# All gate matmuls of an attention step in one block, between the transposes of its two pairs

## The chip, the cores and the metric

One core of a Trainium2 chip runs the whole program. The metric is the device time of one execution in microseconds (us). TensorE (PE) does the matmuls and the transposes, ScalarE (ACT) and VectorE (DVE) the element-wise work, SyncE (SP) and GpSimd (POOL) issue transfers. The loads of the stationary operand are recorded apart from the matmuls, as PEld. Engines run their own instruction lists in order and wait for each other on semaphores.

## What is computed

One layer of a transformer on 128 context tokens and 512 latent tokens, model width 1024. Cut to what matters here:

```
u = h @ w_in  -> A: q(8 heads) k,v(2 heads) | B: q,k,v(8 heads) | gate_A | gate_B
ya = attention A   (window of +-128 tokens, a sink logit, keys of the cache)
yb = attention B   (8 x 16 neighbourhood on the 64-wide grid with a bias, keys of the cache)
merge = (sigmoid(gate_A) * (ya @ w_out_a) + sigmoid(gate_B) * (yb @ w_out_b)) @ w_o
x = x + gate1 * merge;  x = x + gate2 * SwiGLU(...)
```

The gates need only h and their columns of w_in, so their matmuls can stand anywhere before the merge. This kernel puts most of them into the attention, as work for TensorE while the other engines do the softmax.

## The kernel before, in words

The attention is a list of 40 pairs (`PAIRS`). A pair is one mixer, one tile of two heads (`hh` = 0 and 1) and one block of 128 queries. Mixer A has the first 20 pairs, mixer B the last 20. Two pairs make a step, a = 2i and b = 2i + 1, so there are 20 steps (`N_STEPS`); the text counts them from 1 to 20. For each pair:

- `scores` (L2378), TensorE: queries by keys into PSUM. It is run two steps ahead.
- `negate_scores` (L1610), VectorE: mask or bias, negated, and the row minimum.
- `exp` (L1072), ScalarE; then `normalise` (L1618 reciprocal, L1622 scaling of the two heads), VectorE.
- `transposes` (L2390), TensorE: each head's probabilities are turned, in blocks of 128 keys: 1, 3 or 4 blocks by the pair. The blocks of one head go into one PSUM bank (4 + hh). It waits for `norm_done` of the head, and for `pt_done` of the pair before it, since that pair used the same bank.
- `copy_pt` (L1080), ScalarE: one copy per head from PSUM to SBUF, which signals `pt_done`.
- `outputs` (L2406), TensorE: probabilities by values. Each head's first matmul waits for its `pt_done`. `take_output` (L1090, L1094) on ScalarE copies the result.

The gate matmuls are cut into chunks `(g, half, k)` of three matmuls 128x320 (L2418). `GATE_STEPS[i]` says which chunks belong to step i: 4 chunks in 14 steps and 8 in 6 steps (numbers 3, 8, 13, 16, 19 and 20). When a half of a gate is complete, ScalarE takes it with `take_gate` (L1062).

The order on each engine is written out by hand. TensorE's is the loop below, ScalarE's in one step is: two copies of a, one `exp` of the next step's a, two copies of b, two more `exp`, the gate if one is complete, the last `exp`, the two outputs, and in six steps a 1.06 us split of weights (L887). So the copies of b stand behind an `exp` that itself waits for VectorE, and three `exp` of the next step stand behind the copies of b. VectorE does in one step the four `negate_scores` of the next step, `normalise` of its two pairs, in most steps one or two parts of a modulation sum (L1464), and in six steps a split (L1413).

TensorE's loop in the kernel before (L2433 to L2446):

```
for i in range(N_STEPS):
    a, b = 2 * i, 2 * i + 1
    n = len(GATE_STEPS[i]) // 2
    transposes(a)
    for chunk in GATE_STEPS[i][:n]: gate_chunk(*chunk)
    transposes(b)
    for chunk in GATE_STEPS[i][n:]: gate_chunk(*chunk)
    outputs(a); outputs(b)
    if i + 2 < N_STEPS: scores(a + 4); scores(b + 4)
```

The numbers of blocks of pairs a and b come from `value_parts`. Over the 20 steps they are (a, b): (1, 4) in steps 1 and 6, (3, 4) in 2 and 7, (1, 3) in 11 and 16, (3, 3) in 5, 10, 12, 14, 15, 17, 19 and 20, (4, 1) in 3 and 8, (4, 3) in 4 and 9, (3, 1) in 13 and 18.

Of the kernel before, what the change touches and what calls it, by code (L numbers as in the profile page):

```python
# [230 lines left out]
def hybrid_dit_program(nc, x_t, c_t, w_ada1, w_ada, w_main, vecs, consts, cache_ka,  # L231
# [6 lines left out]
    with ctx:  # L238
# [293 lines left out]
        GATE_STEPS, CHUNKS = [], [(g, half, k) for g in range(N_GATE_ATT) for half in range(2) for k in range(KT)]  # L532
# [1631 lines left out]
        def _(pe):  # L2164
# [202 lines left out]
            def scores(p):  # L2367
                mixer, t, blk = PAIRS[p]
                if p >= 2:
                    pe.wait_ge(ttr_done, 2 * p - 2)  # L2370

                parts = [score_parts(mixer, t, blk, hh) for hh in range(2)]
                tile = (QA if mixer == "A" else QB) + t
                for c in range(len(parts[0])):
                    for hh in range(2):
                        rows = slice(hh * HD, (hh + 1) * HD)
                        at, keys = parts[hh][c]
                        ins = pe.matmul(ps[:, 2 * (p % 2) + hh, at:at + keys.shape[1]], qk[rows, tile, blk * P:(blk + 1) * P],  # L2378
                                        keys, start=True, stop=True)
                        if c == len(parts[0]) - 1:  # L2380
                            ins.then_inc(score_done, 1)

            def transposes(p):
                for hh in range(2):
                    r = 2 * p + hh
                    if p:
                        pe.wait_ge(pt_done, r - 1)
                    pe.wait_ge(norm_done, r + 1)
                    for c, (at, n, _) in enumerate(value_parts(*PAIRS[p], hh)):
                        ins = pe.transpose(ps[0:n, 4 + hh, c * P:(c + 1) * P], e_sb[r % 8][:, at:at + n], ident)  # L2390
                    ins.then_inc(t_done, 1)

            def outputs(p):

                parts = [value_parts(*PAIRS[p], hh) for hh in range(2)]
                if p >= 2:
                    pe.wait_ge(o_done, p // 2 * 2)
                if p == FIRST_B:
                    pe.wait_ge(v_in, 16 * 3)
                    pe.wait_ge(pool_set, 2)  # L2400
                for c in range(len(parts[0])):
                    for hh in range(2):
                        if c == 0:
                            pe.wait_ge(pt_done, 2 * p + hh + 1)
                        _, n, v = parts[hh][c]
                        ins = pe.matmul(ps[hh * HD:(hh + 1) * HD, 6, p % 2 * P:(p % 2 + 1) * P], v,  # L2406
                                        pt_sb[PAIRS[p][0]][p % 2][hh][0:n, c * P:(c + 1) * P],
                                        start=c == 0, stop=c == len(parts[0]) - 1)
                ins.then_inc(pv_done, 1)

            def gate_chunk(g, half, k):
                if k == 0:
                    if not half:
                        pe.wait_ge(lo_done, U_GATE + g + 1)
                    pe.wait_ge(act_read, N_ACC + 2 * g + half)
                w = slice(k * P, (k + 1) * P)
                for n, (wt, rt) in enumerate(((w_hi, h_hi), (w_hi, h_lo), (w_lo, h_hi))):
                    ins = pe.matmul(ps[:, 7, 0:TH], wt[:, (U_GATE + g) % RING, w], rt[:, k, half * TH:(half + 1) * TH],  # L2418
                                    start=k == 0 and n == 0, stop=k == KT - 1 and n == 2)
                if k == KT - 1:  # L2420
                    ins.then_inc(pe_unit if half else first_half, 1)
# [10 lines left out]
            scores(3)  # L2432
            for i in range(N_STEPS):  # L2433
                a, b = 2 * i, 2 * i + 1
                n = len(GATE_STEPS[i]) // 2
                transposes(a)
                for chunk in GATE_STEPS[i][:n]:
                    gate_chunk(*chunk)
                transposes(b)
                for chunk in GATE_STEPS[i][n:]:  # L2440
                    gate_chunk(*chunk)
                outputs(a)
                outputs(b)
                if i + 2 < N_STEPS:
                    scores(a + 4)
                    scores(b + 4)  # L2446
# [313 lines left out]
```

## Time and profile before

| what | us |
|---|---|
| median of 3 runs (894.14 to 897.92) | 894.8 |
| the profiled execution, its own time | 894.82 |
| its span in the trace | 893.0 |
| PE busy / DVE busy / ACT busy | 877.5 / 706.5 / 468.0 |
| the attention, from the first scores to the last outputs | 164.6 to 298.0 |

Busy time of PE counts overlapping matmuls as they are drawn in the trace, so it hides small gaps. How densely TensorE works is seen better in the starts of its weight loads (PEld rows): one starts per matmul, 0.146 us apart in a gate block. A row's columns are start, duration (from the first start to the last end, when several instructions are merged), engine, line, operation, operands, count, and in brackets the idle time before it and what ended that.

### The profile page before, as it was taken

How to read it: one execution, taken by the hardware profiler on the slowest of the kernel's cores; microseconds unless marked ns; L12 is line 12 of the kernel's file. 1: busy time of each engine (PE TensorE's matmuls, PEld its weight loads, DVE VectorE, ACT ScalarE, POOL GpSimd, SP SyncE). 2: the span in 40 equal slices, each digit the busy share in tenths (PEclk: the TensorE clock that was granted, in tenths of full speed). 3: DMA queues.
4: the chain of work that ended last, by engine and by line, in shares of the span. 5: the costliest groups of instructions: out<-in, count | busy, mean ns of one | idle time of the engine just before them, and what ended most of it. 6: DMA issues, size and time to landing. Idle time of an engine off the chain costs nothing. (4 is left out here: it accounts for less than half of the span.)

```text
span 893.0 us, 16552 instructions
## 1 busy us (share of the span) xinstructions
PE 877.5 (98%) x6235; PEld 833.9 (93%) x6235; DVE 706.5 (79%) x1330; ACT 468.0 (52%) x973; POOL 122.3 (14%) x155
## 2 busy tenths in 40 slices
PE   6999999999999999999999999999999999999998
PEld 5689888898889999999998999999999999999997
DVE  4657899799788499774777968997777998778887
ACT  4763444777777533432246734555444555545553
POOL 0000000010000000000000123223333222333221
PEclk9999999999999999999999999999999999999999
DMA  9954344441453220228305478878989886898867
GB/s 366 364 190 166 139 141 143 143 134 62 153 157 117 72 71 1 78 112 328 120 24 214 98 163 188 189 168 195 204 190 201 189 188 164 193 214 188 183 150 146
DMA packets 51663, 145.32 MB, mean 163 GB/s; under 512 B 6000, under 2 KB 12416, under 8 KB 50176
## 3 DMA queue, kind: packets, MB, share of 16 engines
q1 hardware_dynamic: 32000, 102.38, 34.8%
q0 software_dynamic: 18864, 41.11, 24.1%
q8 instruction: 50, 0.82, 0.4%
q10 hardware_dynamic: 720, 0.77, 0.3%
q14 instruction: 29, 0.24, 0.1%
HBM read 121.68 MB, written 12.20 MB: 150 GB/s over the span
## 5 line engine op out<-in xcount | busy, mean ns | idle before, releaser
L1318 ACT ACTIVATE w_hi<-stage 128x512 fp32r<-128x512 f32 (+1 forms) x186 | 106.0, 608 | 98.4 <-DMA stage<-stage 47.8
L2009 DVE TENSOR_TENSOR w_lo<-stage,w_hi 128x512 fp32r<-128x512 f32 (+1 forms) x186 | 117.7, 668 | 25.2 <-ACT w_hi L1318 24.9
L2608 PE MATMUL ps<-m_hi,w_hi 128*128 128x320 f32 x304 | 93.9, 309 | 0.0
L2608 PE MATMUL ps<-m_lo,w_hi 128*128 128x320 f32 x304 | 93.9, 309 | 0.0
L2608 PE MATMUL ps<-m_hi,w_lo 128*128 128x320 f32 x304 | 93.9, 309 | 0.0
L2608 PE MATMUL ps<-h_hi,w_hi 128*128 128x320 f32 x272 | 84.0, 309 | 0.0
L2608 PE MATMUL ps<-h_lo,w_hi 128*128 128x320 f32 x272 | 84.0, 309 | 0.0
L2608 PE MATMUL ps<-h_hi,w_lo 128*128 128x320 f32 x272 | 84.0, 309 | 0.0
L887 ACT ACTIVATE w_hi<-stage 128x1024 fp32r<-128x1024 f32 x47 | 49.6, 1064 | 62.2 <-PE ps L2278 36.9
L2608 PE MATMUL ps<-y_hi,w_hi 128*128 128x320 f32 x264 | 81.7, 309 | 0.0
L2608 PE MATMUL ps<-y_lo,w_hi 128*128 128x320 f32 x264 | 81.6, 309 | 0.0
L2608 PE MATMUL ps<-y_hi,w_lo 128*128 128x320 f32 x264 | 81.6, 309 | 0.0
L1413 DVE TENSOR_TENSOR w_lo<-stage,w_hi 128x1024 fp32r<-128x1024 f32 x47 | 57.2, 1221 | 30.1 <-ACT w_hi L887 29.7
L2278 PE MATMUL ps<-w_hi,h_hi 128*128 128x512 f32 (+1 forms) x200 | 75.0, 375 | 0.0
L2278 PE MATMUL ps<-w_lo,h_hi 128*128 128x512 f32 (+1 forms) x200 | 73.7, 369 | 0.0
L2278 PE MATMUL ps<-w_hi,h_lo 128*128 128x512 f32 (+1 forms) x200 | 73.7, 368 | 0.0
L2608 PEld LDWEIGHTS ps<-m_lo,w_hi 128*128 128x128 f32 x304 | 57.1, 188 | 0.0
L2608 PEld LDWEIGHTS ps<-m_hi,w_lo 128*128 128x128 f32 x304 | 57.1, 188 | 0.0
L2608 PEld LDWEIGHTS ps<-m_hi,w_hi 128*128 128x128 f32 x304 | 57.1, 188 | 0.0
L2608 PEld LDWEIGHTS ps<-h_hi,w_hi 128*128 128x128 f32 x272 | 51.1, 188 | 0.0
L2608 PEld LDWEIGHTS ps<-h_lo,w_hi 128*128 128x128 f32 x272 | 51.1, 188 | 0.0
L2608 PEld LDWEIGHTS ps<-h_hi,w_lo 128*128 128x128 f32 x272 | 51.1, 188 | 0.0
(311 smaller groups left out, 2440.0 us busy)
## 6 DMA issues: line engine op xcount, KB each, us to landing
stage<-w_main SPq DMA_DIRECT2D x118, 512.0 KB, 4.3
x<-w_ada SPq DMA_DIRECT2D x21, 512.0 KB, 4.6
stage<-stage POOLq DMA_DIRECT2D x38, 256.0 KB, 4.3
qk<-w_ada SPq DMA_DIRECT2D x7, 1024.0 KB, 12.0
scr<-w_main POOLq DMA_DIRECT2D x28, 256.0 KB, 6.1
y_t<-scr POOLq DMA_DIRECT2D x22, 320.0 KB, 6.5
s_second<-w_main POOLq DMA_DIRECT2D x26, 256.0 KB, 6.2
stage<-w_main POOLq DMA_DIRECT2D x19, 256.0 KB, 6.6
```

The source lines that it names most:

```text
L887: act.activation(w_hi[:, slot, :], stage[:, slot, :], ACT.Copy).then_inc(hi_done, 1)
L1318: act.activation(w_hi[:, slot, at:at + job_half(j) * P], left_stage(op, j), ACT.Copy).then_inc(left_hi[op], 1)
L1413: dve.tensor_tensor(w_lo[:, slot, :], stage[:, slot, :], w_hi[:, slot, :].bitcast(F32), ALU.subtract).then_inc(lo_done, 1)
L2009: dve.tensor_tensor(w_lo[:, slot, w], left_stage(op, j), w_hi[:, slot, w].bitcast(F32), ALU.subtract).then_inc(left_lo[op], 1)
L2278: ins = pe.matmul(ps[:, acc_bank(b, i), 0:width], (h_hi, h_lo)[part][:, k, i * P:(i + 1) * P], wt[:, u % RING, at:at + width], start=k == ...
L2608: ins = pe.matmul(ps[:, BANK_OF[op], 0:TH], wt[:, slot, w], right(op, part, j, k), start=k == 0 and n == 0, stop=k == half - 1 and n == 2)
```

## The change

The gate chunks of a step are no longer halved around the second pair's transposes. All of them stand between the transposes of a and the transposes of b; nothing stands between the transposes of b and the outputs. Chunks, their number per step and their order are the same.

```
@@ -2432,13 +2432,10 @@
             scores(3)
             for i in range(N_STEPS):
                 a, b = 2 * i, 2 * i + 1
-                n = len(GATE_STEPS[i]) // 2
                 transposes(a)
-                for chunk in GATE_STEPS[i][:n]:
+                for chunk in GATE_STEPS[i]:
                     gate_chunk(*chunk)
                 transposes(b)
-                for chunk in GATE_STEPS[i][n:]:
-                    gate_chunk(*chunk)
                 outputs(a)
                 outputs(b)
                 if i + 2 < N_STEPS:
```

TensorE's list in step 1, from the last matmul of the first half's gate chunks to the first matmuls of the outputs (L2418 gate matmuls, L2390 transposes, L2406 values). Before:

```order
L2418 MATMUL ps<-h_hi,w_lo 128x320
L2390 MATMUL ps<-cst,scr 128x128 x8
L2418 MATMUL ps<-h_hi,w_hi 128x320
L2418 MATMUL ps<-h_lo,w_hi 128x320
L2418 MATMUL ps<-h_hi,w_lo 128x320
L2418 MATMUL ps<-h_hi,w_hi 128x320
L2418 MATMUL ps<-h_lo,w_hi 128x320
L2418 MATMUL ps<-h_hi,w_lo 128x320
L2406 MATMUL ps<-x,va 64x128
L2406 MATMUL ps<-pt_end,va 64x128
```

After:

```order
L2418 MATMUL ps<-h_hi,w_lo 128x320
L2418 MATMUL ps<-h_hi,w_hi 128x320
L2418 MATMUL ps<-h_lo,w_hi 128x320
L2418 MATMUL ps<-h_hi,w_lo 128x320
L2418 MATMUL ps<-h_hi,w_hi 128x320
L2418 MATMUL ps<-h_lo,w_hi 128x320
L2418 MATMUL ps<-h_hi,w_lo 128x320
L2390 MATMUL ps<-cst,scr 128x128 x8
L2406 MATMUL ps<-x,va 64x128
L2406 MATMUL ps<-pt_end,va 64x128
```

The eight transposes of pair b move behind six gate matmuls, next to the outputs. The same on TensorE in step 3, where each half has twelve gate matmuls and pair b one block per head, at the end of the gate work. Before:

```order
L2418 MATMUL ps<-h_hi,w_hi 128x320
L2418 MATMUL ps<-h_lo,w_hi 128x320
L2418 MATMUL ps<-h_hi,w_lo 128x320
L2406 MATMUL ps<-x,va 64x128
L2406 MATMUL ps<-pt_end,va 64x128
```

After:

```order
L2418 MATMUL ps<-h_lo,w_hi 128x320
L2418 MATMUL ps<-h_hi,w_lo 128x320
L2390 MATMUL ps<-cst,scr 128x128 x2
L2406 MATMUL ps<-x,va 64x128
L2406 MATMUL ps<-pt_end,va 64x128
```

Here the two transposes move behind twelve gate matmuls. The lists of ScalarE, VectorE, SyncE and GpSimd are the same in both kernels, and TensorE's is the same outside the 20 steps.

## Rows read from the trace of the kernel before

**Rows 1.** The page: TensorE's busy time, and its granted clock in 40 slices.
```profile
PE 877.5 (98%) x6235; PEld 833.9 (93%) x6235; DVE 706.5 (79%) x1330; ACT 468.0 (52%) x973; POOL 122.3 (14%) x155
...
PEclk9999999999999999999999999999999999999999
```

**Rows 2.** Busy time by stretch: attention, the stage behind it, the feed-forward.
```profile
core 0: us, PE busy (x) PEld busy (x) DVE busy (x) ACT busy (x) POOL busy (x), PEclk, DMA share, GB/s
164.60:298.00 133.40, 132.88 (x1346) 119.32 (x1345) 112.39 (x354) 98.38 (x300) 2.91 (x3) 1.00 0.41 129
298.00:456.00 158.00, 158.00 (x1079) 158.00 (x1078) 120.08 (x169) 57.84 (x84) 0.00 (x0) 1.00 0.31 111
...
494.00:889.70 395.70, 394.75 (x2691) 394.40 (x2690) 327.48 (x560) 203.06 (x395) 116.11 (x142) 1.00 0.81 179
```

**Rows 3.** Who the weight loads waited for, attention: us, times, longest us.
```profile
PEld ps L2390 <- ACT pt_end L1080: 0.5, 1, 0.5
```

**Rows 4.** Timeline of weight loads, step 5 (blocks 3 and 3, four chunks).
```profile
198.18 0.64 PEld L2390 LDWEIGHTS ps<-cst,scr 128*128 128x128 f32 x6 [0.33 <-issue]
198.79 0.19 PEld L2418 LDWEIGHTS ps<-h_hi,w_hi 128*128 128x128 f32 x1
...
199.62 0.72 PEld L2390 LDWEIGHTS ps<-cst,scr 128*128 128x128 f32 x6
200.32 0.19 PEld L2418 LDWEIGHTS ps<-h_hi,w_hi 128*128 128x128 f32 x1
...
201.40 0.13 PEld L2406 LDWEIGHTS ps<-x,va 128*64 128x64 f32 x1 [0.19 <-issue]
...
202.86 0.30 PEld L2378 LDWEIGHTS ps<-cka,qk 64*128 64x128 f32 x4 [0.17 <-issue]
```

**Rows 5.** Timeline of ScalarE, step 5: the two copies of pair b.
```profile
200.30 0.87 ACT L1080 ACTIVATE vf<-ps 128x384 f32<-128x384 f32 x2 [0.28 <-PE ps L2390]
```

**Rows 6.** Timeline, step 6 (1 and 4 blocks): transposes and copies of pair b.
```profile
205.60 0.94 PEld L2390 LDWEIGHTS ps<-cst,scr 128*128 128x128 f32 x8
...
206.54 1.06 ACT L1080 ACTIVATE vf<-ps 128x512 f32<-128x512 f32 x2
```

**Rows 7.** Timeline, step 7 (3 and 4 blocks): VectorE, weight loads, ScalarE.
```profile
211.52 0.88 DVE L1622 TENSOR_SCALAR scr<-scr,small 128x512 f32<-128x512 f32 x2
...
212.12 0.86 PEld L2390 LDWEIGHTS ps<-cst,scr 128*128 128x128 f32 x8 [0.49 <-ACT pt_end L1080]
...
213.89 1.06 ACT L1080 ACTIVATE vf<-ps 128x512 f32<-128x512 f32 x2
...
214.02 0.13 PEld L2406 LDWEIGHTS ps<-x,cva 128*64 128x64 f32 x1 [0.19 <-issue]
...
216.02 0.30 PEld L2378 LDWEIGHTS ps<-qk 64*128 64x128 f32 x4 [0.17 <-issue]
```

**Rows 8.** Timeline, steps 11 and 18: transposes and copies of pair b.
```profile
238.57 0.72 PEld L2390 LDWEIGHTS ps<-cst,scr 128*128 128x128 f32 x6
...
239.72 0.85 ACT L1080 ACTIVATE pt_end<-ps 128x384 f32<-128x384 f32 x2
...
281.35 0.29 PEld L2390 LDWEIGHTS ps<-cst,scr 128*128 128x128 f32 x2
...
282.20 0.42 ACT L1080 ACTIVATE pt_end<-ps 128x128 f32<-128x128 f32 x2
```

**Rows 9.** Timeline, steps 19 and 20: scalings, transposes of pair a, copies of b.
```profile
284.29 0.68 DVE L1622 TENSOR_SCALAR scr<-scr,small 128x320 f32<-128x320 f32 x2
...
285.12 0.64 PEld L2390 LDWEIGHTS ps<-cst,scr 128*128 128x128 f32 x6 [0.23 <-issue]
...
287.44 0.72 PEld L2390 LDWEIGHTS ps<-cst,scr 128*128 128x128 f32 x6
...
288.44 0.85 ACT L1080 ACTIVATE pt_end<-ps 128x384 f32<-128x384 f32 x2
...
290.12 0.75 DVE L1622 TENSOR_SCALAR scr<-scr,small 128x384 f32<-128x384 f32 x2
...
291.56 0.53 PEld L2390 LDWEIGHTS ps<-cst,scr 128*128 128x128 f32 x5 [0.17 <-issue]
```

More of the change, by code:

```diff
@@ L2434, in _ @@
                 a, b = 2 * i, 2 * i + 1
-                n = len(GATE_STEPS[i]) // 2
                 transposes(a)
-                for chunk in GATE_STEPS[i][:n]:
+                for chunk in GATE_STEPS[i]:
                     gate_chunk(*chunk)
                 transposes(b)
-                for chunk in GATE_STEPS[i][n:]:
-                    gate_chunk(*chunk)
                 outputs(a)
```

## The prediction, made before the changed kernel was run

> **What bounds the kernel now.** I read the page first: TensorE is busy 877.5 of 893.0 us at a granted clock of 1.00 [rows 1]. Then the busy time by stretch: in the attention TensorE has 132.88 of 133.40 us, and from its end to 456 us it is never idle, nor nearly ever in the feed-forward [rows 2]. So the end is set by TensorE's list, and whatever TensorE gains or loses in the 20 attention steps reaches the end one for one. The work that follows the attention on the other engines hangs on the last outputs and moves with them.
>
> Third, what TensorE waited for in the attention: the view of waits has one of note, 0.5 us [rows 3]. It is at the second pair's transposes of step 7, and the timeline corrects the engine named: the scaling of pair b's first head started at 211.52 and two took 0.88, so the first ended at about 212.00, and the transposes began at 212.12 [rows 7]. VectorE ended that wait, 0.53 us. A second is in the outputs of the same step. Seven blocks at 0.21 us and a seam of 0.20 (both below) make 1.67 us, and they took 214.02 to 216.02 = 2.00: 0.33 us, the second copy of b being late. All else is issue, and the gate chunks behind the transposes of b are what makes it so: they run while ScalarE copies.
>
> Last, one plain step, number 5 [rows 4]. Transposes of a 198.18 to 198.79 = 0.61; six gate matmuls to 199.62 = 0.83; transposes of b to 200.32 = 0.70; six gate matmuls to 201.40 = 1.08; outputs of six blocks to 202.86 = 1.46. The second gate block is longer than the first by 0.24: a seam where the weight tile goes from 128x128 to 128x64. The outputs have six blocks at 0.21 and a seam of 0.20 in front of the scores.
>
> **The change, part by part.** No instruction is added or removed. Five terms.
>
> (1) *Issue time.* Old: 0.61 + 0.83 + 0.70 + 1.08 = 3.22 us. New: 0.61, twelve gate matmuls 0.83 + 0.88 = 1.71 (six more at 0.146), transposes 0.70, and a seam from transposes to outputs that the trace does not have. Its nearest rows: no seam at all from transposes to gates (bound 0), 0.20 from outputs to scores, 0.24 from gates to outputs. I take 0.20, since the last matmul before it is as short (128 columns) as the last of the outputs, and the gate matmul has 320. New: 3.22. Nothing changes, and the eight-chunk steps add the same 0.88 twice. With 0 it would be -4.0 us over 20 steps, but the term below would take most back; with 0.24, +0.8 at most. Here a rule of the Trainium skill can be weighed ("TensorE: Matmul & The Clock Gate", section "Measured speedup vs the span model"): a weight load overlaps running matmuls only when it goes to another group of rows. These rows disagree: loads of 0.19 us start every 0.146 us on the same 128 rows. Taken at its word it would make the new seam as dear as the dearest, +0.8 us.
>
> (2) *The copies of b lose their cover.* From the first load of b's transposes to the first copy: 199.62 to 200.30 = 0.68 us with three blocks [rows 4, 5]; four blocks add one pitch of 0.11, one block takes off two, so 0.79 and 0.45. The two copies then take 0.87 (three blocks), 1.06 (four) [rows 6], 0.42 (one) [rows 8], and TensorE sees the last after 0.05 us. So the outputs of b may be complete in their needs 1.60, 1.90 or 0.92 us after that first load. TensorE arrives there after the transposes (0.70, 0.91, 0.26), the seam of 0.20 and the outputs of a, 0.21 per block; before the change also after 0.88 or 1.75 us of gates. The wait per step now:
> (1, 4) blocks: 1.90 - 1.32 = 0.58, two steps, 1.16;
> (3, 4): 1.90 - 1.74 = 0.16, two steps, 0.32;
> (1, 3): 1.60 - 1.11 = 0.49, two steps, 0.98;
> (3, 3): 1.60 - 1.53 = 0.07, eight steps, 0.56;
> (4, 1), (4, 3), (3, 1): none (cover left over: 0.38, 0.14 and 0.17), six steps.
> Sum +3.0 us. The (3, 3) steps are on the edge: an error of 0.05 us in the handover is 0.4 us in the sum.
>
> (3) *ScalarE late for its own reasons.* The copies of b stand behind an exponential that waits for VectorE. Before, the copy began later than the transposes allowed by 206.54 - 205.60 - 0.79 = 0.15 in step 6 [rows 6], 213.89 - 212.12 - 0.79 = 0.98 in step 7 [rows 7], 239.72 - 238.57 - 0.68 = 0.47 in step 11 and 282.20 - 281.35 - 0.45 = 0.40 in step 18 [rows 8]. The transposes of b now come 0.88 later, which would seem to hide this. But in the step before the copies of b also came 0.88 later against the next transposes of a, and all of ScalarE's and VectorE's chain behind them. The two cancel, and the lateness shrinks only by what TensorE stood still in the step before. Step 6: 0.15 - 0.07 = 0.08. Step 7: 0.98 + 0.53 (its transposes no longer wait) - 0.66 = 0.85. Step 11: 0.47 - 0.07 = 0.40. Step 18: 0.40 - 0.07 - 0.17 of cover left = 0.16. Sum +1.5 us.
>
> (4) *New waits at the transposes of a.* By the same shift the scaled probabilities of the next step have 0.88 us less (1.75 behind an eight-chunk step) minus what the step waited. Steps 19 and 20 are where that is not there. Step 19: scaling of the first head done at about 284.29 + 0.38, seen 0.08 later, transposes at 285.12: 0.37 spare; 0.88 - 0.16 - 0.37 = +0.35. Step 20: done at 290.12 + 0.42 + 0.08, transposes at 291.56, 0.94 spare; step 19's copies had been 288.44 - 287.44 - 0.68 = 0.32 late, which goes: 1.75 - 0.07 - 0.94 - 0.32 = +0.42 [rows 9]. Sum +0.8 us. The other steps have over 1.3 us spare, or follow a step that waits (7 and 12).
>
> (5) *The two old waits go.* They are now in the new ones: -0.53 - 0.33 = -0.86 us [rows 7].
>
> Also moved, at no cost: a complete half gate is ready one set of transposes earlier, so its copy on ScalarE is never late; weight splits and transfers keep their place in their queues, and wait for the same gates.
>
> Sum: 0 + 3.0 + 1.5 + 0.8 - 0.9 = +4.4 us. The profiled execution took 894.82 (span 893.0 and 1.8 around it), which is the median of 894.8, so **899.2 us**, 0.5% slower. I moved all 20 steps in this way; the bounds are: seam 0 instead of 0.20, -1.0 us (the waits of 14 steps grow by 0.20 and give 2.8 of 4.0 back, and the nearly waiting ones some more); handover 0.1 us shorter or longer, about -1.2 to +1.4; term 3 nothing, or undiminished by earlier waits, -1.5 to +0.9. Together some 897 to 901.5.
>
> **The rivals.**
> *Hidden after all.* Only the steps with a short pair a or a long pair b wait (1.16 + 0.32 + 0.98), ScalarE's lateness is absorbed by the later transposes, and the old waits go: 894.8 + 2.5 - 0.9 = 896.4. For it: ScalarE was idle 0.28 us ahead of b's copies in step 5 [rows 5] and would be more so. Against it: the 0.07 us margins.
> *Faster.* An unbroken gate block saves the 0.24 seam 20 times, the transposes drain without a seam, and the outputs of a cover the copies: 894.8 - 4.8 - 0.9 = 889.1. It decides at the first outputs of b: they would have to be ready 1.33 us after the transposes' first load, and the copies alone end at 1.55. I give it little.
> *A lasting lag.* ScalarE's chain never recovers: in each of the other 16 steps b's copies come some 0.40 us late as in step 11, +6.4 us, 905.6. Against it: in step 5 ScalarE waits for TensorE, and would wait 0.88 us more.
> *The clock.* It is 1.00 in every slice [rows 1, 2], through stretches with no gate matmul: outputs, scores, transposes. These grow by the transposes of b and the waits, about 1 us. No row is at the lower of its two levels, 1.2 GHz; if the twelve gate matmuls of a step took twice their 1.75 us, six such steps would add 10.5 us to the forecast, 909.7. The Trainium skill ("TensorE: Matmul & The Clock Gate", section "Part 4: PE-mode transpose") says transposes do not count as activity for the clock. The old trace shows no fall around them.
> *The change not done:* the instruction lists show it done.
>
> **How the numbers follow.** Forecast and its bounds 0.76, hidden 0.09, lasting lag 0.10, faster 0.03, clock 0.02. The range that leaves out two in ten runs from 896.8 to 901.8. A measurement of this kernel tells about 0.5% (4.5 us) from no change, that is 899.3, so the forecast lies on the border: within 0.5% 0.50 (half of the forecast's share, a little more, and the hidden case), slower 0.47, faster 0.03.
>
> **What would show it.** The transposes of b directly ahead of the outputs, their first loads 0.20 us beyond the pitch apart; a weight load waiting for a copy (L1080) in 14 to 16 steps, largest in steps 1, 6, 7, 11 and 16; the transposes of step 7 no longer waiting; waits of 0.3 to 0.4 us at the first transposes of steps 19 and 20; the attention ending at 302.4 instead of 298.0, and everything behind it as long as before. Wrong, if the (3, 3) steps wait 0.2 us or more or not at all, if the seam is not 0.20, or if the time behind the attention changes.

## The result, and the profile after

The changed kernel took 903.2 us, median of six executions (900.1 to 907.3), against 895.5 us for six of the kernel before beside it: a ratio of 1.0085 (95% interval 1.0062 to 1.0108). It is slower, as forecast, but the time lies 4.0 us above the forecast of 899.2 and above the range, which ended at 901.8.

The page of the changed kernel answers to [rows 1]: TensorE is busy 6.4 us more, the span is 8.7 us longer. The granted clock is 9 or more tenths in all 40 slices, as before.

```profile
PE 883.9 (98%) x6235; PEld 838.5 (93%) x6235; DVE 707.5 (78%) x1330; ACT 466.4 (52%) x973; POOL 123.0 (14%) x155
```

To find where 8.7 us lie I cut both traces at the same two instructions of TensorE's list: the first weight load of the scores just ahead of step 1's transposes, and the first load behind the last outputs (L2170). Between them lie the 20 steps; this stretch is "the attention" from here on. The timelines of weight loads, first before, then after:

```profile
170.11 0.30 PEld L2378 LDWEIGHTS ps<-cka,qk 64*128 64x128 f32 x4 [0.19 <-issue]
...
297.99 0.30 PEld L2170 LDWEIGHTS ps<-h_hi,w_hi 128*128 128x128 f32 x2 [0.17 <-issue]
```

```profile
171.60 0.30 PEld L2378 LDWEIGHTS ps<-cka,qk 64*128 64x128 f32 x4 [0.19 <-issue]
...
305.13 0.30 PEld L2170 LDWEIGHTS ps<-h_hi,w_hi 128*128 128x128 f32 x2 [0.17 <-issue]
```

127.88 us before, 133.53 after: **+5.65**, where the working said +4.4. The change also starts the attention 1.49 us later, and TensorE's last weight load starts 591.84 us behind the attention's end (896.97 - 305.13) instead of 590.31 (888.30 - 297.99), +1.53. Nothing was changed there. Busy time by stretch, columns as in [rows 2], for 3.4 us ahead of the attention and 3.4 us behind it, and the weight loads at the start of the second:

```profile
19.50:22.90 3.40, 3.40 (x22) 3.10 (x25) 1.75 (x5) 0.30 (x1) 0.65 (x1) 0.51 0.99 408
483.70:487.10 3.40, 3.40 (x15) 3.40 (x14) 2.37 (x4) 2.25 (x3) 0.57 (x1) 0.50 0.92 283
```

```profile
483.15 0.19 PEld L2534 LDWEIGHTS ps<-h_hi,w_hi 128*128 128x128 f32 x1 [0.69 <-DVE w_lo L1413]
...
483.71 0.33 PEld L2534 LDWEIGHTS ps<-h_lo,w_hi 128*128 128x128 f32 x1
483.98 0.33 PEld L2534 LDWEIGHTS ps<-h_hi,w_lo 128*128 128x128 f32 x1
484.25 0.33 PEld L2534 LDWEIGHTS ps<-h_hi,w_hi 128*128 128x128 f32 x1
```

The granted clock is 0.50, that is 1.2 GHz, and loads start every 0.27 us (483.71, 483.98, 484.25) instead of every 0.146. An estimate from these rows: 3.4 x (1 - 0.146 / 0.267) = 1.5 us lost, twice. TensorE had waited 0.69 us for a weight split just before the second; the same wait stands in the trace of before, at full clock. In the attention itself the clock is 1.00.

Next the view of waits in the attention of the changed kernel (us in total, times, longest); before, it had one wait of note [rows 3]:

```profile
PEld ps L2406 <- issue: 5.9, 25, 0.9
PEld ps L2390 <- issue: 4.9, 14, 0.7
```

In the kernel before the first two were 3.7 (longest 0.2) and 4.1 (longest 0.3). Most of the new idle time is under "issue", though the timeline shows that it ends when a copy does. Step 5, weight loads (answers to [rows 4]), and those of step 7, the transposes of pair b and the outputs that wait for its copies (answers to [rows 7]):

```profile
201.75 0.19 PEld L2418 LDWEIGHTS ps<-h_hi,w_hi 128*128 128x128 f32 x1
...
203.47 0.72 PEld L2390 LDWEIGHTS ps<-cst,scr 128*128 128x128 f32 x6
204.37 0.13 PEld L2406 LDWEIGHTS ps<-x,va 128*64 128x64 f32 x1 [0.17 <-issue]
```

```profile
216.80 0.94 PEld L2390 LDWEIGHTS ps<-cst,scr 128*128 128x128 f32 x8
217.91 0.13 PEld L2406 LDWEIGHTS ps<-x,cva 128*64 128x64 f32 x1 [0.17 <-issue]
...
219.06 0.19 PEld L2406 LDWEIGHTS ps<-vf,va 128*64 128x64 f32 x2 [0.51 <-issue]
219.48 0.13 PEld L2406 LDWEIGHTS ps<-vf,va 128*64 128x64 f32 x1 [0.23 <-ACT vf L1080]
```

Step 5: gates 201.75 to 203.47 = 1.72, transposes with their seam 0.90 = 0.70 + 0.20. That is the working's 1.71 and 0.20 to 0.01. Step 7: the transposes of b wait no more, the outputs wait 0.51 and 0.23 for the two copies.

I then took each step's length apart (transposes, gates, transposes, outputs, scores) in both traces. Two places differ from the working, steps 4 and 6. Step 4 has blocks (4, 3) and was to wait for nothing. Its outputs before and after:

```profile
195.20 0.13 PEld L2406 LDWEIGHTS ps<-x,va 128*64 128x64 f32 x1 [0.19 <-issue]
...
196.88 0.52 PEld L2378 LDWEIGHTS ps<-qk 64*128 64x128 f32 x8 [0.17 <-issue]
```

```profile
197.49 0.13 PEld L2406 LDWEIGHTS ps<-x,va 128*64 128x64 f32 x1 [0.17 <-issue]
...
198.73 0.45 PEld L2406 LDWEIGHTS ps<-vf,cva 128*64 128x64 f32 x3 [0.38 <-issue]
...
199.84 0.52 PEld L2378 LDWEIGHTS ps<-qk 64*128 64x128 f32 x8 [0.17 <-issue]
```

1.68 and 2.35 us. Followed back, the copies of b start late because the exponential ahead of them (L1072) waited 1.40 us for VectorE; and VectorE was late because the two scalings of pair b, step 4's second pair, had taken 2.11 us instead of 0.75. GpSimd was copying at that moment. ScalarE, VectorE and GpSimd, step 4, after:

```profile
197.53 0.62 ACT L1072 ACTIVATE scr<-scr,small 128x385 f32<-128x385 f32 x1 [1.40 <-DVE small L1610]
...
198.14 0.85 ACT L1080 ACTIVATE vf<-ps 128x384 f32<-128x384 f32 x2
```

```profile
193.39 1.28 DVE L1464 CUSTOM_DVE_ANT_0 x<-x,bb,vec 128x1024 f32<-128x1024 f32 x1
...
194.79 2.11 DVE L1622 TENSOR_SCALAR scr<-scr,small 128x384 f32<-128x384 f32 x2
196.82 0.66 DVE L1610 CUSTOM_DVE_ANT_0 scr<-ps,amask,small 128x384 f32<-128x384 f32 x1
```

```profile
194.18 1.39 POOL L807 COPY qk<-bb 128x1024 f32<-128x1024 f32 x1 [173.17 <-PE ps L2378]
195.51 1.18 POOL L807 COPY cossin<-bb 128x1024 f32<-128x1024 f32 x1
196.63 1.15 POOL L809 MEMSET vbz<- 64x1024 f32 x1
```

And before, GpSimd and VectorE:

```profile
191.94 1.03 POOL L807 COPY qk<-bb 128x1024 f32<-128x1024 f32 x1 [170.83 <-PE ps L2378]
...
193.91 0.94 POOL L809 MEMSET vbz<- 64x1024 f32 x1
```

```profile
190.80 0.75 DVE L1622 TENSOR_SCALAR scr<-scr,small 128x384 f32<-128x384 f32 x2
191.47 0.67 DVE L1610 CUSTOM_DVE_ANT_0 scr<-ps,amask,small 128x384 f32<-128x384 f32 x1
```

GpSimd's two copies (bb, the broadcast vector, into two buffers that had become free) and a memset are released by step 3's scores, so by TensorE. They moved by 194.18 - 191.94 = 2.24 us: 1.49 for the later start, and the 0.73 that TensorE waited in steps 1 and 2. The scalings hang on exponentials behind the copies of b of step 3, and moved by 194.79 - 190.80 = 3.99: the same 2.24 and the 1.75 of twelve gate matmuls that now stand ahead of b's transposes. Before, VectorE's scalings ended at 191.55, 0.39 us ahead of GpSimd's first copy at 191.94. The change slid them onto it. The working had followed what waits for what, and had not compared these two movements.

### The profile page after: what moved, and what is told of

The parts are those of the page before. It is cut to its first block and busy times, and to the rows that moved or that the text cites. A ratio compares the mean times of both kernels' runs of the same rounds, so it can differ in the third digit from the quotient of the medians.

```text
span 901.7 us, 16552 instructions
## 1 busy us (share of the span) xinstructions
PE 883.9 (98%) x6235; PEld 838.5 (93%) x6235; DVE 707.5 (78%) x1330; ACT 466.4 (52%) x973; POOL 123.0 (14%) x155
## 5 line engine op out<-in xcount | busy, mean ns | idle before, releaser
L1413 DVE TENSOR_TENSOR w_lo<-stage,w_hi 128x1024 fp32r<-128x1024 f32 x47 | 57.2, 1221 | 29.2 <-ACT w_hi L887 28.9
L1072 ACT ACTIVATE scr<-scr,small 128x513 f32<-128x513 f32 (+5 forms) x80 | 46.2, 583 | 12.5 <-DVE small L1610 12.5
```

What stands on the lines that cost most here:

```text
L1072: act.activation(e_sb[r % 8][:, lo:end], s_neg[r % 8][:, lo:end], ACT.Exp, bias=nmax[:, r % 8:r % 8 + 1], scale=-1.0, accum_out=rsum[:, r ...
L1413: dve.tensor_tensor(w_lo[:, slot, :], stage[:, slot, :], w_hi[:, slot, :].bitcast(F32), ALU.subtract).then_inc(lo_done, 1)
```

## The experiments

All lengths of the attention are from the profiled execution, between the two instructions above. Of the kernel before and of the changed kernel there are two traces each, and their lengths agreed to 0.01 us, so these lengths carry the argument; each other kernel has one trace. Ratios are against the kernel before on the same chip.

**Both kernels again.** No edit.

> The kernel before, unchanged, timed beside the others. The changed kernel's profiled execution was 8.7 us longer than the one of before: 5.65 in the attention, 1.49 ahead of it (one stretch of 3.4 us at half the TensorE clock, at 19.5 us) and 1.5 behind it (another, at 483.7 us). Theory A: such half-clock stretches fall into executions of either kernel by chance and have nothing to do with the change; then some executions of this kernel show a mean clock of 0.995 to 0.998 too, each stretch some 1.5 us, and its fastest is 894.1, its attention 127.9 us from the second scores to the end. Theory B: the change brings them; then this kernel shows 0.999 or more in every execution.

> The changed kernel again. Attention 133.5 us where before has 127.9 (+5.65), the same in every profile if it is set by the order of work. Theory A (chance of the clock): the fastest executions lie 5.5 to 6.0 us above the fastest of before, the median 5.5 to 8. Theory B (the change brings slow clock): no execution at 0.999, median 7 to 9 above.

The kernel before: 897.2 us (median of 12, 894.6 to 901.0), ratio to itself 1.001 (0.999 to 1.003), attention 127.89. The changed kernel: 903.0 (median of 12, 900.0 to 906.5), ratio 1.007 (1.0047 to 1.0094), attention 133.52. So the longer attention is the kernel's own: +5.65 in the first two traces, +5.63 in these. The times around it are not: the second trace of the changed kernel had no stretch at half clock before TensorE's last matmul, and its execution took 900.07; that of the kernel before had one of 6.8 us at 24.7 us, and its attention began 2.6 us later. The fastest executions stand 5.8 us apart (894.2 of 35, 900.0 of 12), about what the attention gained. The rest of a median goes with such stretches, which either kernel has in some executions: two medians of the kernel before, timed together on one chip (895.97 of 35, and 897.19 of 12), are 1.2 us apart. So the theory that the change alone brings such stretches fails: 10 of these 12 executions had a mean granted clock of 0.998 or less.

**GpSimd held back in the changed kernel.** One wait is added, so that its copies start when both pairs of step 4 have been scaled (`norm_done` at 16, eight pairs of two heads):

```
             pool.wait_ge(rope_done, 5)
+            pool.wait_ge(norm_done, 16)
             for v in range(2):
                 ins = nc.gpsimd.tensor_copy(cbc_late[v], ...)
```

> The changed kernel, but GpSimd's two copies (L807) and its memset wait until VectorE has scaled the eighth pair, so they run beside score reductions and not beside L1622. Theory 1 (collision): in step 4 of the changed kernel two scalings of VectorE took 2.11 us instead of 0.75 while GpSimd copied; VectorE was then late in step 4 (0.73 us of new waits of TensorE) and still in step 6 (0.63 beyond the forecast). Without it the attention is 132.2 us (133.5 - 1.36), near the +4.4 of the forecast. Theory 2 (the chain of ScalarE and VectorE alone): steps 4 and 6 stay as they are, 133.5.

900.2 us (median of 12), ratio 1.0054 (1.0033 to 1.0074), attention 132.17, as expected. The collision is gone, and 1.35 us of the attention with it (133.52 - 132.17). VectorE's groups by shape, with this run between the kernel before and the changed one (x32, busy us, mean ns; lines count one higher in this run):

```profile
L1622 DVE TENSOR_SCALAR scr<-scr,small 128x384 f32<-128x384 f32 x32 | 12.0, 418 | 0.6
```

```profile
L1623 DVE TENSOR_SCALAR scr<-scr,small 128x384 f32<-128x384 f32 x32 | 12.0, 418 | 0.6
```

```profile
L1622 DVE TENSOR_SCALAR scr<-scr,small 128x384 f32<-128x384 f32 x32 | 13.4, 460 | 0.6
```

In the changed kernel VectorE lost 2.11 - 0.75 = 1.36 us in two instructions, and TensorE as much. Step 4's outputs lose 0.67 of it. Step 6's show nearly all the rest; with GpSimd held back they run 207.70 to 209.64:

```profile
207.70 0.13 PEld L2407 LDWEIGHTS ps<-x,va 128*64 128x64 f32 x1 [0.17 <-issue]
...
209.64 0.30 PEld L2379 LDWEIGHTS ps<-qk 64*128 64x128 f32 x4 [0.17 <-issue]
```

1.94 us. In the changed kernel they run 210.62 to 213.15 = 2.53:

```profile
210.62 0.13 PEld L2406 LDWEIGHTS ps<-x,va 128*64 128x64 f32 x1 [0.17 <-issue]
...
213.15 0.30 PEld L2378 LDWEIGHTS ps<-qk 64*128 64x128 f32 x4 [0.17 <-issue]
```

**The collision put into the kernel before.** The same line of GpSimd's list, but it waits for `exp_done` at 18, the exponentials of the ninth pair. So GpSimd starts together with the scalings of step 5's first pair, one pair later than where the changed kernel collides. TensorE's order is untouched.

> The kernel before, but GpSimd's copies wait until the two exponentials of the ninth pair's heads are done, so that they start as VectorE scales. If scalings and GpSimd's copies exclude each other, one pair of scalings takes 1.5 to 2.5 us instead of 0.75. With the old cover of gate matmuls TensorE should hardly notice: attention 127.9 to 128.6. If they do not exclude each other, all scalings stay at 0.75.

898.4 us (median of 10), ratio 1.0028 (1.0001 to 1.0054), attention 129.68, +1.80. The long scalings came as expected, but the cost was a miss, since I had expected 0.7 us at most. The collision took in both pairs of step 5, and the cover did not absorb it. VectorE and GpSimd in this run:

```profile
199.96 2.31 DVE L1623 TENSOR_SCALAR scr<-scr,small 128x384 f32<-128x384 f32 x2
...
202.37 1.33 DVE L1623 TENSOR_SCALAR scr<-scr,small 128x384 f32<-128x384 f32 x2
```

```profile
199.91 1.03 POOL L808 COPY qk<-bb 128x1024 f32<-128x1024 f32 x1 [179.75 <-ACT scr L1073]
200.89 1.17 POOL L808 COPY cossin<-bb 128x1024 f32<-128x1024 f32 x1
202.00 1.16 POOL L810 MEMSET vbz<- 64x1024 f32 x1
```

The four scalings took 2 x 0.75 = 1.50 us before and take 3.64 here, 2.14 more. Before, VectorE had idled 0.24 us between the two pairs; the split of weights behind them (L1413, here L1414) starts 29.35 us into the attention instead of 27.54, so VectorE is 1.81 us late, and TensorE lost 1.80 with all gate chunks where they were. I had taken cover for the thing that decides. But in these steps VectorE's own work is the chain: in the kernel before it had no idle time of note from that split to step 7, where TensorE already waited 0.53 us for a scaling [rows 7].

**The change in six steps only** (those where I expected most: 1, 2, 6, 7, 11, 16), and **in the fourteen others only**.

```
-                n = len(GATE_STEPS[i]) // 2
+                n = len(GATE_STEPS[i]) // (1 if i in (0, 1, 5, 6, 10, 15) else 2)
```

> The new order only in steps 1, 2, 6, 7, 11 and 16, where pair a has one block or pair b four; the other 14 as before. Theory of the prediction (copies of b lose their cover, priced by blocks): the waits of these steps, 0.58 + 0.15 + 0.58 + 0.15 + 0.49 + 0.47 = 2.4 us, less the old waits of step 7 (0.86), plus what ScalarE is late by in steps 7 and 11: attention 127.9 + 2.1 = 130.0 us, and no stretched scaling on VectorE. A rival, that the cost comes from the seam between transposes and values: 6 x 0.2 of 20 x 0.2 saved or lost alike, attention within 0.3 us of before.

> The complement: the new order in the 14 steps whose blocks give the copies just enough cover (margins of 0 to 0.4 us). By blocks alone it would cost 8 x 0.04 = 0.3 us. But ScalarE's and VectorE's chain still comes 0.88 us later in every such step, and the steps between, with the old order, have no new wait that would give it time: my replay of the lists gives +3.0 us, most of it as waits for scaled probabilities and late copies, and +1.4 more if the scaling of pair 8 meets GpSimd's copies again. Attention 128.2 (blocks alone), 130.9 (chain), 132.3 (chain and collision).

Six steps: 898.3 us (median of 10), ratio 1.0025 (1.0001 to 1.0049), attention 130.07, +2.19. GpSimd starts at 192.25 and its copies take 1.03 and 1.04: no collision, since step 3 is as before. Fourteen steps: 902.0, ratio 1.0056 (1.0032 to 1.0081), attention 132.28, +4.40, with scalings of 2.10 us for two. The six came out as priced by blocks (130.0 expected). The fourteen are far above the 128.2 that blocks alone gave, and cost twice as much as the six. Whether that was the chain or the collision was left to a run of its own:

**The fourteen steps, GpSimd held back.**

> As fourteen_steps_only (whole gate block ahead of the second pair's transposes in 14 steps, halved in steps 1, 2, 6, 7, 11 and 16), with GpSimd's two copies (L807) and memset held back until step 4's scaling is signalled. That run's attention took 132.28 us, 4.40 more than the kernel before, and the collision of GpSimd and VectorE was read in it (one scaling of 1.19 us). Theory (chain of waits plus collision): with the GpSimd work late the collision's 1.36 us go, as between changed_again and changed_pool_late: attention 130.9, no scaling (L1622) over 0.5 us. Rival (the 4.40 us are the chain of waits alone, and the long scaling hides in spare time): attention 132.3. A small third: the GpSimd work meets VectorE later instead, 131.5 or so with a long scaling in step 5.

897.4 us (median of 10, 897.2 to 898.4), ratio 1.001 (0.9992 to 1.0027), attention 130.96, +3.08 instead of +4.40. This is what the chain of waits gave once the collision was taken out (130.9). Six (+2.19) and fourteen (+3.08) together make +5.27, more than the whole change without the collision (+4.29): the waits are not additive. As I read it, a step that waits gives the next one time, which is what terms 3 and 4 of the working were about.

**One chunk left behind the transposes of b**, then the same **with GpSimd held back**.

```
+                n = len(GATE_STEPS[i]) - 1
                 transposes(a)
-                for chunk in GATE_STEPS[i]:
+                for chunk in GATE_STEPS[i][:n]:
                     gate_chunk(*chunk)
                 transposes(b)
+                for chunk in GATE_STEPS[i][n:]:
+                    gate_chunk(*chunk)
```

> All gate chunks of a step but one stand between the transposes, the last (0.44 us) behind those of b. If the lost cover is what costs, each wait for a copy shrinks by 0.44 and the seam grows by 0.03: (1, 4) steps 0.1, (1, 3) steps 0.05 to 0.1, (3, 4) and (3, 3) none; attention 129.4 (+1.5), of which most is ScalarE late in steps 7 and 11 and the waits of steps 19 and 20; up to 130.7 if GpSimd's copies are met. If the cost were all or nothing, it stays at 133.5 or falls to 127.9.

> As one_chunk_behind (all gate chunks but the last ahead of the second pair's transposes, one chunk of 0.44 us behind them), with GpSimd's copies and memset held back until step 4's scaling is signalled. That run's attention took 130.93 us where the lists moved without a collision gave 129.4. Theory (the difference is the collision): attention 129.4 to 129.7, no scaling over 0.5 us. Rival (one chunk as cover is worth less than the lists say): attention stays near 130.9. If the theory holds, one chunk behind the transposes takes back 2.5 of the 4.3 us that the chain of waits costs.

899.0 us (ratio 1.003, 1.0006 to 1.0054), attention 130.93; then 899.5 (ratio 1.0037, 1.001 to 1.0063), attention 129.47. The medians don't tell these two apart, the attention does: 1.46 us of collision. The second one's fastest execution took 895.8, its slowest 903.1; a median of ten can hide 1.5 us here. One chunk of 0.44 us as cover takes back 132.17 - 129.47 = 2.7 of the 4.29 us; the (3, 3) steps' outputs and those of steps 2 and 16 no longer wait, and step 1's wait 0.15 us.

**Scores as cover.** In the changed kernel the scores of the step after next stand between the transposes of b and the outputs.

```
                 transposes(b)
+                if i + 2 < N_STEPS:
+                    scores(a + 4)
+                    scores(b + 4)
                 outputs(a)
                 outputs(b)
-                if i + 2 < N_STEPS:
-                    scores(a + 4)
-                    scores(b + 4)
```

> The gate block unbroken as in the changed kernel, but the scores of two steps ahead stand between the transposes of b and the values: 1.0 to 1.7 us of other work as cover for the copies of b. The waits for copies of b should go (3 us), VectorE gets its scores earlier; the transposes of the next a follow the values directly, and the last two steps have no scores. If seams cost as before: attention 127.9 to 130.5. If it is under 127.0 it beats both kernels.

900.3 us, ratio 1.0042 (1.002 to 1.0065), attention 132.30: a miss, since I had expected 127.9 to 130.5. The waits for copies went, and a new one took their place: scores need PSUM that VectorE must have read. The view of waits in the attention:

```profile
PEld ps L2378 <- DVE small L1610: 5.3, 12, 0.9
PEld ps L2390 <- issue: 4.9, 21, 0.7
PEld ps L2406 <- issue: 3.9, 14, 0.3
```

A collision was in it too: one 128x512 scaling took 1.26 us instead of 0.48, and the sum behind it (L1464) 2.05 instead of 1.28, 1.55 us of VectorE's time in all. No run took the two apart.

```profile
191.59 2.05 DVE L1464 CUSTOM_DVE_ANT_0 x<-x,bb,vec 128x1024 f32<-128x1024 f32 x1
```

**ScalarE's copies first.** In the changed kernel the first `exp` of the next step stands behind both copies of b, so that nothing of VectorE's can hold them up.

```
-                if more:
-                    exp(a + 2, 0)
                 copy_pt(b, 0)
                 copy_pt(b, 1)
                 if more:
+                    exp(a + 2, 0)
```

> The changed kernel with ScalarE's order altered in every step: the first exponential of the next step stands behind both copies of the second pair instead of ahead of them. Term 3 of the prediction (copies of b late because they stand behind an exponential that waits for VectorE, 1.5 us) would go if that were all: attention 133.5 - 1.5 = 132.0 or less. My lists, moved in the new order, say the other way: that exponential comes some 1.3 us later, VectorE's scaling of the next first pair with it, and TensorE waits at the transposes of a instead: attention 1.6 us longer, 135.1. Collision as in the changed kernel in both.

903.1 us (median of 6), ratio 1.0073 (1.005 to 1.0097), attention 135.29, where 135.1 was expected. The collision is in it too (two scalings took 2.10 us). Its waits in the attention:

```profile
PEld ps L2389 <- issue: 9.0, 17, 1.3
PEld ps L2405 <- issue: 3.9, 23, 0.2
```

The outputs (L2405) wait less than in the changed kernel, 3.9 instead of 5.9, and the transposes (L2389) much more, 9.0 instead of 4.9. So the copies can be had earlier, but at a price: the exponential that stood in front of them starts the chain to the next step's transposes, and these now wait up to 1.3 us.

## Why the prediction was right in its waits and wrong in its time

- **What bounds the kernel.** Right. TensorE's list sets the end: its last weight load comes 590.3 us behind the attention in both kernels where no stretch ran at half clock. The prediction had named a change behind the attention as a sign of being wrong; the first trace has one of 1.53 us, and it is the clock.
- **Issue time, 0.** Right. The new seam measured 0.20 us; no gain, no loss. The rule that the working weighed here stands in the Trainium skill ("TensorE: Matmul & The Clock Gate") under "The mechanism", one section above the one it named; the 0.24 us that the working drew from it is not what came.
- **Copies lose their cover, +3.0.** Right where the blocks are uneven: 0.58 in step 1, 0.15 in step 2, 0.47 in step 16 (0.58, 0.16, 0.49 forecast). The (3, 3) steps wait 0.04 instead of 0.07, 0.2 us less over eight steps.
- **ScalarE late, +1.5.** Right: with the collision out, step 6 waits 0.69 in both terms together (0.66 forecast), step 7 0.91 (1.01), step 11 0.86 (0.89), step 18 0.15 (0.16).
- **New waits at the transposes of a, +0.8.** Step 19 +0.35, step 20 +0.51 (0.35 and 0.42), by the idle time in front of their transposes of a against [rows 9], 0.58 - 0.23 and 0.68 - 0.17:

```profile
291.65 0.64 PEld L2390 LDWEIGHTS ps<-cst,scr 128*128 128x128 f32 x6 [0.58 <-issue]
...
298.64 0.64 PEld L2390 LDWEIGHTS ps<-cst,scr 128*128 128x128 f32 x6 [0.68 <-issue]
```

- **The old waits go.** Right, the transposes of step 7 don't wait. Without the collision the five terms came to 132.17 - 127.88 = +4.29 instead of +4.4.
- **"Also moved, at no cost: ... weight splits and transfers keep their place in their queues."** This is the first step that failed. It looked at places in queues and at the gates that they wait for, and not at GpSimd's three element-wise instructions, which stood in [rows 2] as 2.91 us of POOL in the attention. Their order is unchanged; what they run beside is not. That cost 1.36 us (133.53 - 132.17): 0.67 at the outputs of step 4 and 0.06 at its transposes, 0.59 at the outputs of step 6, hundredths elsewhere.
- **The sum against the time.** This is the second step that failed. The forecast was put on top of 894.8, the median of three and the time of an execution without a stretch at half clock, and the clock was given nothing, because it is 1.00 in every slice of that one trace [rows 1, 2]. With the collision the working gives 894.8 + 4.4 + 1.4 = 900.6, and the fastest executions of the changed kernel took 900.0 to 900.1: both lie inside the range. What took the median of six out of it is the other 2.6 us. They go with the stretches at half clock, of which the profiled execution had two, 1.5 us each: in order of time the six took 900.1, 901.7, 903.0, 903.5, 905.7 and 907.3 us, with mean granted clocks of 0.999, 0.999, 0.996, 0.995, 0.994 and 0.989. The kernel before has them too: with 35 executions its median is 896.0 and not 894.8.
- **What stays open.** Whether the change makes such stretches a little more frequent: against 896.0 the twelve executions of the changed kernel have +7.0, 1.3 more than the attention's +5.65, and two medians of one kernel lay 1.2 apart. A mean granted clock of 0.999 or more was had by 5 of 18 executions of the changed kernel and by 17 of 47 of the kernel before that were timed beside its second twelve, but by all ten with the fourteen steps and GpSimd held back. No run shows why.
- **The rivals.** Hidden after all, and faster: no, the (3, 3) steps do wait, though little. A lasting lag: no, no wait in steps 8 to 10 and 12 to 15 is over 0.04 us. The clock: as the prediction meant it, no, it stayed at 1.00 in the 20 steps, through the longer stretches without gate matmuls; the stretches at 1.2 GHz lie elsewhere.

## What to carry to other kernels

When a change shifts one engine's work against another's, list what runs *at the same moment* on VectorE and GpSimd, before and after, and not only what waits for what; two instructions released by different engines move by different amounts (here 2.24 and 3.99 us), and an old margin of 0.4 us is no margin. Work that covers another engine's round trip should not all stand on one side of it: with GpSimd out of the way the attention took 132.2 us with nothing behind the transposes and 129.5 with one chunk of 0.44 us out of 1.75; halved, it took 127.9. And where executions scatter by 6 us, rest the argument on the length of a stretch between two instructions, which repeats to 0.01 us, and take the level from more than three of them.

## What the runs showed of the hardware

**GpSimd and VectorE shut each other out.** Scalings of 128x384 fp32 in SBUF took 0.42 us alone and up to 1.19 beside a GpSimd copy of 128x1024, which took 1.39 or 1.18 instead of 1.03; the same copies beside VectorE's L1610, which reads PSUM, cost neither anything (0.67, 1.03). The Trainium skill ("SBUF — State Buffer", section "Who interferes with whom") says that the two engines share a pair of ports as an exclusive lock, and that the loser blocks for the other's whole instruction. The trace agrees: the first scaling in the changed kernel, alone in this row, had started 0.78 us ahead of the end of the copy that it met (195.57) and ends 0.21 behind it (195.78). An estimate from these rows: less its own 0.42 us it worked from 195.36 on, when the copy was all but done.

```profile
194.79 0.99 DVE L1622 TENSOR_SCALAR scr<-scr,small 128x384 f32<-128x384 f32 x1
```

VectorE's sum L1464, which reads two tiles in SBUF, is in it too. In the changed kernel the first copy started at 194.18, beside an L1464 that had started at 193.39 and kept its 1.28 us, and took 1.39. The scaling is not what lengthened it: with the collision put into the kernel before, a scaling followed the copy by 0.05 us (199.96 and 199.91), and the copy took 1.03. In the run with ScalarE's copies first (lines count one lower) it started 0.08 us behind one and took 2.09, while L1464 kept its 1.28; in the run with scores as cover L1464 started behind a copy (191.59 and 191.33), and took 2.05. In each of these rows the one that started first kept its time. The memset, which reads nothing, took 0.94 beside an L1464 in the kernel before (193.91 and 193.86), but 1.15 behind a scaling.

```profile
192.45 2.09 POOL L807 COPY qk<-bb 128x1024 f32<-128x1024 f32 x1 [171.58 <-PE ps L2377]
```

```profile
192.37 1.28 DVE L1463 CUSTOM_DVE_ANT_0 x<-x,bb,vec 128x1024 f32<-128x1024 f32 x1
```

**Half clock in some executions.** Stretches of 3.4 us (6.8 in the second trace of the kernel before, 13.7 in the run with the collision put into it) at 1.2 GHz start between 18 and 25 us or between 480 and 501 us in some executions of the kernels here and not in others. Ahead of the one at 483.7 us TensorE had just waited 0.69 us for a weight split; in the traces of the kernel before and in the second of the changed kernel, which have the same wait, it kept its clock. In the first trace of the changed kernel each 3.4 us cost 1.5; the 6.8 us made the attention begin 2.6 later, the 13.7 us 4.2. No run here controlled them.
